# Byte positions of the moving matmul operands in SBUF, relative to the weights, in steps of 4 bytes

## The reference, cut to what matters

```
x = x + pool_attn_mixer(rms_norm(x))       # w_in 1024x2048, w_out 1024x1024
x = x + conv_ffn(rms_norm(x))              # w_in 1024x5632, w_out 2816x1024   (layer 0)
x = x + rglru_mixer(rms_norm(x))           # w_in 1024x2560, w_out 1280x1024
x = x + conv_ffn(rms_norm(x))              # the same shapes as before         (layer 1)
h = rms_norm(x) * (1 + sc1) + sh1          # second_block; sc, sh, gt come from c @ ada_w
x = x + gt1 * (sum of 4 gated mixers of h @ w_in) @ w_o
x = x + gt2 * (relu(h2 @ ffn_w1) ** 2) @ ffn_w2      # 1024x4096, 4096x1024
out = rms_norm(x)
```

## Time and profile before

| | us |
|---|---|
| median of three runs | 1091.65 |
| the three runs | 1098.56, 1091.49, 1091.65 |
| the profiled execution | 1097.18 |
| its span, first to last instruction | 1095.3 |
| TensorE busy in it | 1055.0 |

### The profile page before, as it was taken

One profiled execution on the slowest core, in us unless ns is written; L12 is line 12 of the kernel. 1 busy time (PEld: TensorE's weight loads), 2 busy tenths in 40 slices (PEclk: granted clock), 3 DMA queues, 4 the chain that ended last, 5 costly groups with the idle time before them and its releaser, 6 DMA issues.

```text
span 1095.3 us, 20957 instructions
## 1 busy us (share of the span) xinstructions
PE 1055.0 (96%) x8608; PEld 1000.8 (91%) x8608; DVE 831.2 (76%) x1418; ACT 626.0 (57%) x1056; POOL 72.0 (7%) x79
## 2 busy tenths in 40 slices
PE   7999999999999989999999997999999999999996
PEld 7876999999998879999999987899989989999996
DVE  6456899888888878988798789998975687755452
ACT  7545686666556846766655693222333467976440
POOL 0322200000102001000000100000000021000010
PEclk8999999999999989999999999899999999999998
DMA  8459465556677854767776542222434265566651
GB/s 341 133 174 313 168 196 189 193 169 188 188 237 231 289 191 154 256 225 256 246 216 201 190 159 92 62 92 90 144 107 150 83 240 174 194 193 193 194 170 39
DMA packets 59422, 200.39 MB, mean 183 GB/s; under 512 B 6720, under 2 KB 10432, under 8 KB 59200
## 3 DMA queue, kind: packets, MB, share of 16 engines
q1 hardware_dynamic: 57600, 194.54, 55.0%
q10 hardware_dynamic: 1728, 4.53, 1.1%
HBM read 197.99 MB, written 1.05 MB: 182 GB/s over the span
## 4 chain that ended last, share of the span: by engine, by line
PE 85%; DVE 8%; ACT 4%; DMA 2%; issue 1%; ACTq 0%; SPq 0%; POOL 0%; DVEq 0%
PE ps L481 84%; DVE wlo L1575 1%; ACT whi L1051 1%; DVE rst L1608 1%; DMA ring<-rg_w_out 1%; DVE raw L1575 1%; ACT L1051 1%; DVE hl L1575 1%; ACT raw L1051 1%; ACT hh L1051 1%; DMA ring<-pa_w_in 1%; DMA ring<-w_o 0%; DVE bks L1575 0%; DMA ring<-pa_w_out 0%; PE ps L666 0%
## 5 line engine op out<-in xcount | busy, mean ns | idle before, releaser
L481 PE MATMUL ps<-hh,whi 128*128 128x256 f32 (+1 forms) x1656 | 474.5, 287 | 4.9 <-DVE wlo L1575 4.2
L481 PE MATMUL ps<-hh,wlo 128*128 128x256 f32 (+1 forms) x1656 | 463.9, 280 | 0.0
L481 PE MATMUL ps<-hl,whi 128*128 128x256 f32 (+1 forms) x1656 | 463.9, 280 | 0.0
L1575 DVE TENSOR_TENSOR wlo<-ring,whi 128x1024 fp32r<-128x1024 f32 (+2 forms) x314 | 376.7, 1214 | 56.7 <-ACT whi L1051 56.1
L1051 ACT ACTIVATE whi<-ring 128x1024 fp32r<-128x1024 f32 (+2 forms) x314 | 320.9, 1037 | 63.1 <-PE ps L481 41.6
L481 PEld LDWEIGHTS ps<-hh,whi 128*128 128x128 f32 x1656 | 313.9, 190 | 26.0 <-issue 15.8
L481 PEld LDWEIGHTS ps<-hl,whi 128*128 128x128 f32 x1656 | 315.3, 190 | 1.3 <-issue 1.0
L481 PEld LDWEIGHTS ps<-hh,wlo 128*128 128x128 f32 x1656 | 314.6, 190 | 0.0
L481 PE MATMUL ps<-hidh,whi 128*128 128x256 f32 x608 | 169.1, 278 | 0.0
L481 PE MATMUL ps<-hidh,wlo 128*128 128x256 f32 x608 | 169.0, 278 | 0.0
L481 PE MATMUL ps<-hidl,whi 128*128 128x256 f32 x608 | 169.0, 278 | 0.0
(11 more groups left out here) (365 smaller groups left out, 1325.1 us busy)
## 6 DMA issues: line engine op xcount, KB each, us to landing
ring<-ffn_w_in SPq DMA_DIRECT2D x88, 512.0 KB, 3.6
ring<-ffn_w SPq DMA_DIRECT2D x64, 512.0 KB, 4.4
ring<-w_in SPq DMA_DIRECT2D x51, 512.0 KB, 3.4
ring<-ada_w SPq DMA_DIRECT2D x48, 512.0 KB, 4.4
ring<-ffn_w_out SPq DMA_DIRECT2D x32, 448.0 KB, 3.4
ring<-rg_w_in SPq DMA_DIRECT2D x20, 512.0 KB, 4.5
ring<-ffn_w_out SPq DMA_DIRECT2D x16, 512.0 KB, 3.6
ring<-pa_w_in SPq DMA_DIRECT2D x15, 512.0 KB, 7.3
```

Of the source, the lines that this page charges most:

```text
L481: return e.matmul(o, l, r, start=start, stop=stop)
L1575: return e.tensor_tensor(o, a, b, op)
```

## The change

No instruction is added or removed, and no wait. Only places in SBUF change. A helper `parts` allocates a family's two tiles as one tensor with 32 elements to spare and starts them `off` elements in, so that a tile can begin at any multiple of 4 bytes:

```diff
+        def parts(stack, name, rows, pitch, off):
+            both = alloc(stack, name, [128, 2 * rows * pitch + 32], F32R)
+            return [both[:, off + n * rows * pitch:off + (n + 1) * rows * pitch].rearrange("p (k t) -> p k t", k=rows) for n in range(2)]
...
-        hh = alloc(ctx, "hh", [128, 8, T + 128], F32R)
-        hl = alloc(ctx, "hl", [128, 8, T + 128], F32R)
+        alloc(ctx, "fill", [128, 112])
+        hh, hl = parts(ctx, "h", 8, T + 128, 12)
...
-        alloc(ctx, "fill", [128, 80])
+        alloc(ctx, "fill", [128, 64])
...
-        alloc(st, "fill", [128, 48])
-        pah = alloc(st, "pah", [128, 8, T], F32R)
-        pal = alloc(st, "pal", [128, 8, T], F32R)
+        alloc(st, "fill", [128, 32])
+        pah, pal = parts(st, "pa", 8, T, 17)
...
-        alloc(st, "fill", [128, 112])
-        hidh = [alloc(st, "hidh", [128, 22, T], F32R)] * 2
-        hidl = [alloc(st, "hidl", [128, 22, T], F32R)] * 2
+        alloc(st, "fill", [128, 96])
+        hid = parts(st, "hid", 22, T, 20)
+        hidh, hidl = [hid[0]] * 2, [hid[1]] * 2
...
-        alloc(st, "fill", [128, 112])
-        yh = alloc(st, "yh", [128, 10, T], F32R)
-        yl = alloc(st, "yl", [128, 10, T], F32R)
+        alloc(st, "fill", [128, 96])
+        yh, yl = parts(st, "y", 10, T, 22)
...
-        alloc(st, "fill", [128, 112])
-        hidh[1] = alloc(st, "hidh", [128, 22, T], F32R)
-        hidl[1] = alloc(st, "hidl", [128, 22, T], F32R)
+        alloc(st, "fill", [128, 96])
+        hidh[1], hidl[1] = parts(st, "hid", 22, T, 18)
...
-        alloc(s2, "fill", [128, 88])
-        mgh = alloc(s2, "mgh", [128, 8, T], F32R)
-        mgl = alloc(s2, "mgl", [128, 8, T], F32R)
+        alloc(s2, "fill", [128, 72])
+        mgh, mgl = parts(s2, "mg", 8, T, 10)
...
-        alloc(st, "fill", [128, 112])
-        hid2h = alloc(st, "hidh2", [128, 32, T], F32R)
-        hid2l = alloc(st, "hidl2", [128, 32, T], F32R)
+        alloc(st, "fill", [128, 96])
+        hid2h, hid2l = parts(st, "hid2", 32, T, 14)
```

## The result

The changed kernel takes 1123.0 us (median of 4 runs, 1121.9 to 1124.3), the kernel before 1091.6 (4 runs, 1085.9 to 1098.6). The ratio is 1.028, 95% interval 1.024 to 1.032: slower by 2.8%, where I had forecast 1083 us and a range up to 1098.

A forecast was written before the change was run, and what follows sets the result against it. TensorE's fp32r matmul stream was taken as the bound. Bringing all slow stretches to 113.4 ns would save 13.3 us, 1097.2 to 1083.9, said as 1083 us; other engines' accesses were priced at nothing. Range 1068 to 1098 us.

The forecast's parts named there:

- What bounds the kernel, and where a change of places can act: TensorE, busy 1055.0 of 1095.3 us; places act only on 7416 fp32r matmuls, 7.4 us per nanosecond on each.
- Two rates at one place, chosen where a stretch starts: Matmul stream: 113.4 or 117.8 ns between starts at distance 192, kept from one break of the stream to the next.
- The slow stretches: First conv_ffn (6.4 us), shorter stretches and short columns: 13.3 us above the fast rate, so 1097.2 becomes 1083.9 us.
- The term for 258 columns: Products at 911.7 us: 96 matmuls at 120.6 ns instead of 114.2, priced at 0.6 us of gain.
- The bound on the other side: All 7416 matmuls at 117.8 ns, the slowest long-stretch rate for 256 columns: at most 18.9 us more, 1116 us.
- rival D: More collisions: families at worse places get only the slow rate; 1103 us for hh, 1116 for all; chance 0.13.
- The choice of the middle term: Between minus 29 and plus 19 us, it took all stretches at the fast rate, 1083.9 us; chance 0.43.
- The other engines' accesses cost nothing: VectorE operations on moved tensors priced at nothing; 1% of VectorE's 831 us would be 8 us.
- The Trainium skill's line of 16 bytes: SBUF rows off multiples of 16 in five families would touch 65 lines, not 64; no row showed a penalty.
- the sentence that loading weights does not take read bandwidth from the running matmul: Cited for the rival that places do not matter: time stays at 1091.5 to 1098.6 us; chance 0.17.

The follow-up runs named there:

- the last experiment: Against the timed version with everything on multiples of 64 bytes, only the low weights (`wlo`, with `ring`) were moved 64 bytes further; measured 1116.0 us.

## Why the prediction was wrong

- *What bounds the kernel, and where a change of places can act*: right. The distance between starts of the fp32r matmuls adds some 29 us, the span grew by 26.0, and TensorE's clock and the other engines are as they were. One reading was wrong beside it: the granted clock reads 8 in four of the 40 slices of the earlier trace rows, not in the first alone. It is 1.00 in all the stretches that the sum uses, so nothing hangs on it.
- *Two rates at one place, chosen where a stretch starts*: right, and seen again with all families put back to 192, where one 160 us stretch took the other rate.
- *The slow stretches are worth 13.3 us, with all at the fast rate 1083.9 us*: the sum was nearly right, for a kernel that was not the one to be predicted. The version on multiples of 64 has the fast rate in nearly all of the stream; its profiled execution takes 1086.75 us, so 10.4 of the 13.3 us came. What a matmul takes above 113.3 ns adds up to 13.7 us over the uninterrupted pairs of the kernel before and to 3.4 us there; 2.5 of the 3.4 lie in the first ten matmuls after each break, which the sum had not set apart. The term for 258 columns did not come at all: these matmuls take 120.8 ns before and 120.7 there, and only about half of the 96 in the window at 911.7 have 258 columns. The changed kernel has the fast rate in no stretch.
- *The bound on the other side*: this is the step that failed. "In the other direction the trace shows nothing slower than 117.8 ns ... these are the ends: minus 29 and plus 19 us." All those rows were taken at one place, and I used the slower of its two rates as an end for places that no row showed. The new places have 119.2 (h), 120.0 (second hid, hid2 and mg), 121.3 (pa, y). 1.4 to 3.5 ns above the supposed end, on 6900 of the matmuls, made 1123 of the 1116 that were to be the worst case. (The two ends of rival D are also counted from different times: 1103 from the median, 1116 from the profiled execution. From the median, 18.9 us give 1110.5.)
- *The choice of the middle term*: failed with it. I took the fast rate as the nearest row, and the range and the chances followed. The nearest rows said only what happens at 192. They held one sign that should have weighed more: with 113.4 and 117.8 at one place, with nobody waited for, something inside the stream costs time there, and a change that moves seven families to seven new distances has then seven chances to be worse. Rival D had the mechanism and a chance of 0.13, but its price was capped at 117.8.
- *The other engines' accesses cost nothing*: right. wlo took 1215 ns (1214 before), hid from zg 417 (417), h from raw 424 (422), though their tiles now begin at odd places.
- *The Trainium skill's line of 16 bytes* ("SBUF — State Buffer", Specifications (TRN2)): 176 and 208 are multiples of 16 and are slow as well, 119.2 and 116.6 to 119.2 ns, so this rule does not sort the places. With the weights where the kernel before has them, distances that are odd multiples of 64 bytes have 113.4 to 117.8 ns, even ones 118.6 to 120.0, and all others 116.6 to 121.5. Of the Trainium skill's page "TensorE: Matmul & The Clock Gate" (Part 2: What happens when you issue a matmul), the sentence that loading weights does not take read bandwidth from the running matmul does not lead to what the last experiment shows: on TensorE only the loads read the low weights, and moving these by 64 bytes costs the stream 4.4 ns a matmul.

Open remains what exactly collides, why a stretch can keep one of two rates, why h at 64 takes a rate that hid2 at 64 does not, and whether the version on multiples of 64 owes its fast rate to these multiples, to the 128 bytes between high and low weights, or to both. What the runs show is which whole placings are fast.

## What to carry to other kernels

Where each matmul in float32 formats brings its own weight load and streams only 256 columns, the places of both operands in SBUF are worth up to 7% of the stream (113.3 to 121.3 ns). The placing to start from is the whole one that was timed: everything on multiples of 64 bytes, moving tiles 192 bytes behind the high weights and 64 behind the low ones, modulo 512. Parts of it are no rule by themselves: other odd multiples of 64, with everything on multiples of 64, had 118.9 ns in some stretches. Compute the distance to every tensor that TensorE reads, since spare elements in one buffer shift all that lie behind it, and read the distance from one start to the next, not a matmul's duration. A trace of a kernel with one placing bounds nothing for another placing. When a kernel's runs spread by 1% and two identical stages run at two rates, look for such a stable pair of rates; the placing without the slow one was worth 0.9% here and had half the spread.

## What the runs showed of the hardware that I had not expected

- In most placings the stream has one of a few fixed rates, the two of 192 kept for up to 170 us: 113.3, 116.7, 117.8, 118.3, 118.9, 119.2, 120.0, 122.2 ns. Some drift a little instead, as hid2 at 160 (117.2 to 117.5) and h at 128 (118.5 to 118.9). At 2.4 GHz 113.3 ns are 272 cycles, 117.8 are 848 cycles for three matmuls, and 120.0 are 288.
- With all distances kept (192 to `whi`, 64 to `wlo`), a common shift of weights and moving tiles decides which rate exists: on multiples of 64 only 113.4, 48 bytes into a block of 64 only 117.8. Both rates occur 32 bytes into a block, in kernels that have 192 to `whi` and to `wlo`.
- One and the same move of the moving tile by 16 bytes makes the stream slower with the weights at one place (117.8 to 119.1 ns) and faster with them at another (119.9 to 117.8).
- The fastest rate found, 113.3 ns, is still 2.0 ns above the 111.3 of loads with two moving columns. None of the placings tried reached that.
